# Forgetting attention and mLSTM issued as one stage, the cells of the RWKV solve moved beside the memory attention

## The reference, cut to what matters

```
one_block (forgetting attention, causal, 4 heads):
    s = q k^T * 64^-0.5 + f_t - f_s;  masked;  p = softmax(s);  out = p v
step (mLSTM, 16 chunks of 128 tokens, in sequence):
    log_d = b_t - b_s + i_s;  m_t = max(...)
    s   = (q k^T) * exp(log_d - m_t)
    num = s v + w_inter * (q C);  den = sum(s) + w_inter * (q n)
    h   = num / max(|den|, exp(-m_t));  C, n = decay * (C, n) + (w k)^T v
    then sigmoid(o) * h and an RMS norm per head
memory_attention: q of 2048 tokens against 256 memory rows, softmax, p v
rwkv7_time_mix: a delta rule; the kernel solves it by chunks of 128 and
    needs the inverse of unit lower triangular cells of 32 x 32
```

## Time and profile before

| | us |
|---|---|
| median of 3 runs (4438.66 to 4448.36) | 4440.43 |
| the profiled execution | 4424.24 |
| its span | 4422.5 |
| stage fox, from its first DMA to the next stage's first instruction (1348.8 to 1664.2) | 315.4 |
| stage rwkv_factors (1664.2 to 1837.2) | 173.0 |
| stage mlstm with the cells (1837.2 to 2122.3) | 285.1 |
| stage rwkv_chunks (2122.3 to 2352.4) | 230.1 |
| stage mem (2352.4 to 2474.7) | 122.3 |

### The profile page before, as it was taken

The page is one execution under the profiler, slowest core; times in us unless marked ns, Lnnn a source line. Parts: engine busy times, 40 slices in busy tenths (PEclk is TensorE's granted clock), DMA queues, the critical chain, the costliest instruction groups (busy, mean ns, idle before and its releaser), DMA issues. The chain is left out here.

```text
span 4422.5 us, 41472 instructions
## 1 busy us (share of the span) xinstructions
PE 3479.1 (79%) x14981; PEld 2625.0 (59%) x14981; DVE 1570.1 (36%) x2571; ACT 897.6 (20%) x1351; POOL 706.8 (16%) x731
## 2 busy tenths in 40 slices
PE   5848888799955993345796499689899686999879
PEld 2636666588843661244694288567788233666567
DVE  0113223203243445677454222356000100777613
ACT  1022222211012332201121133321001100333210
POOL 1042222111101000122341322110111000000031
PEclk7669999899987995555898699899999898999989
DMA  5232222322214401111003355322221115455354
GB/s 170 86 124 68 82 65 79 132 71 71 71 44 92 84 17 61 43 36 47 17 12 83 112 186 175 111 95 83 78 76 57 68 36 140 83 111 114 79 167 143
DMA packets 305282, 383.48 MB, mean 87 GB/s; under 512 B 83808, under 2 KB 243232, under 8 KB 290096
## 3 DMA queue, kind: packets, MB, share of 16 engines
q1 hardware_dynamic: 289144, 378.00, 29.3%
q10 hardware_dynamic: 16016, 3.95, 0.5%
HBM read 246.36 MB, written 135.53 MB: 86 GB/s over the span
## 5 line engine op out<-in xcount | busy, mean ns | idle before, releaser
L504 PE MATMUL f_psum_out<-f_x_high,f_w_high 128*128 128x512 f32 x1440 | 569.8, 396 | 97.1 <-DVE f_x_low L482 52.8
L504 PE MATMUL f_psum_out<-f_x_low,f_w_high 128*128 128x512 f32 x1440 | 567.3, 394 | 0.0
L504 PE MATMUL f_psum_out<-f_x_high,f_w_low 128*128 128x512 f32 x1440 | 566.5, 393 | 0.0
L504 PEld LDWEIGHTS f_psum_out<-f_x_high,f_w_high 128*128 128x128 f32 x1440 | 274.8, 191 | 163.4 <-issue 92.0
L504 PEld LDWEIGHTS f_psum_out<-f_x_high,f_w_low 128*128 128x128 f32 x1440 | 274.6, 191 | 57.8
L504 PEld LDWEIGHTS f_psum_out<-f_x_low,f_w_high 128*128 128x128 f32 x1440 | 274.9, 191 | 57.1
L393 PE MATMUL p_psum_proj<-p_w_high,p_h_high 128*128 128x512 f32 x512 | 219.2, 428 | 68.4 <-issue 44.7
L1032 PE MATMUL nbr_psum_o<-nbr_probT,nbr_v 128*128 128x512 f32 (+3 forms) x576 | 238.8, 496 | 18.7 <-ACT nbr_probT L1056 18.7
L393 PE MATMUL p_psum_proj<-p_w_high,p_h_low 128*128 128x512 f32 x512 | 215.1, 420 | 0.0
L393 PE MATMUL p_psum_proj<-p_w_low,p_h_high 128*128 128x512 f32 x512 | 213.8, 418 | 0.0
L490 POOL CAST f_w_high<-f_w 128x1024 fp32r<-128x1024 f32 x45 | 46.8, 1040 | 873.0 <-PE f_psum_out L504 575.3
(11 more groups left out here) (494 smaller groups left out, 6586.1 us busy)
## 6 DMA issues: line engine op xcount, KB each, us to landing
f_w<-in_w_fm SPq DMA_DIRECT2D x45, 512.0 KB, 5.4
ada_w<-in_w_ada SPq DMA_DIRECT2D x6, 2048.0 KB, 16.8
scratch_qkmT<-p_qkT_out SPq DMA_DIRECT2D x32, 384.0 KB, 3.3
scratch_z1T<-f_out SPq DMA_DIRECT2D x10, 1024.0 KB, 4.7
p_z<-scratch_z1T SPq DMA_DIRECT2D x16, 640.0 KB, 5.8
p_xt<-in_x SPq DMA_DIRECT2D x16, 512.0 KB, 4.8
p_staging<-in_w_tok SPq DMA_DIRECT2D x8, 1024.0 KB, 4.8
scratch_hT<-p_h_slot SPq DMA_DIRECT2D x16, 512.0 KB, 5.8
```

The lines of the kernel that those rows point to most:

```text
L504: last = nc.tensor.matmul(self.p_out[b][:, at], self.w_parts[b][w_part][:, k, :], self.x_parts[x_part][:, k, at], start=(k == 0 and i == 0 ...
```

## The change

Four things change. First, the engine programs of a stage become Python generators that yield a place (a number of steps), and `run_together` merges them on each engine by that number; where two have the same, the program named first goes first. Second, fox and mLSTM become one stage, all tiles named `heads_*`: chunk c of mLSTM is cut into hops at places 10c, 10c+1, ... of fox's 160 steps (`TURN = 10`). Third, to fit eight PSUM banks, fox has two banks for scores in place of three and one for units in place of two, and mLSTM has three in place of six: `psum_state` and `psum_num` share the bank of `psum_t`, `psum_inter` that of `psum_max`. Fourth, the cells are solved in the DVE program of the memory attention, two turns in each step from step 10 on, and `mem_attention` takes mLSTM's place between `rwkv_factors` and `rwkv_chunks`. The nbr stage keeps its banks and its order.

```diff
+def interleave(*programs):
+    turns = [[next(p, None), p] for p in programs]
+    while turns := [t for t in turns if t[0] is not None]:
+        turn = min(turns, key=lambda t: t[0])
+        turn[0] = next(turn[1], None)
...
-S_BUFS, M_BUFS, P_BUFS = 3, 2, 4
+P_BUFS = 4
...
+        yield -1
+        dve.wait_ge(const_ready, 1)
...
+        for s in range(n_steps + 4):
+            yield s
+            if aside:
+                aside(dve, s, n_steps)
+            for m in plan.before[s]:
+                largest(m)
+            if s >= 3 and plan.ends_group(s - 3):
+                normalise(plan.group_of(s - 3))
...
+                     extra_ones=[raw(qx[b][HD:HD + 2, :]) for b in range(2)], s_bufs=2, m_bufs=1)
...
+    run_together(nc, attention(nc, d, g, ph, plan, kT, v, 7, load_head, lambda b, q1: q1, lambda b: kT[b], d["y1T"][GW:2 * GW],
+                               aside=cells.eliminate), cells.transfers())
...
+        first = 2 * (s - self.FIRST)
+        for j in range(max(first, 0), min(first + 2, CELL - 1)):
...
+            yield self.FIRST + CELL // 2
+            sp.wait_ge(self.x_done, 1)
...
+    p_state = p_num = p_t
+    p_inter = p_max[:].rearrange("p h t -> p (h t)")
...
+    def on_tensor(pe):
+        yield -2
+        pe.wait_ge(const_in, 48)
+        pe.wait_ge(sel_ready, 1)
+        for h in range(GH):
+            last = nc.tensor.matmul(p_max[:, h, 0:NT], sel[:, h, :], carry_row[:], start=True, stop=True)
...
+            yield TURN * c + 5
+            pe.wait_ge(state_ready, c + 2)
+            pe.wait_ge(sm_ready, c + 1)
...
+            yield TURN * c + 6
+            dve.wait_ge(num_ready, c + 1)
...
-    mlstm(nc, d, g, cells)
+    mem_attention(nc, d, g, cells)
     rwkv_chunks(nc, d, g, big, to_next, cells)
...
-    fox_attention(nc, d, g)
+    ph = Phase(nc, "heads")
+    run_together(nc, fox_attention(nc, d, g, ph), mlstm(nc, d, g, ph))
+    ph.close()
     rwkv(nc, d, g)
-    mem_attention(nc, d, g)
     tile_pass_2(nc, d, g)
```

More of the change, by code:

```diff
@@ new lines, in on_sync, with load @@
+    def on_sync(sp):
+        def load(h):
+            b = h % 2
+            if h >= 2:
+                sp.wait_ge(o_ready, plan.ends[plan.group(h - 2, GROUPS - 1)])
+            load_head(sp, h, b, q1[b], q2[b], head_in[b])
+            if tables:
+                tables.load(sp, h, b)
+        yield -3
+        load(0)
+        load(1)
+        for n in range(n_groups):
+            yield plan.ends[n] + 3
+            h, q = n // GROUPS, n % GROUPS
+            at = slice(h % 2 * HD, h % 2 * HD + HD)
+            sp.wait_ge(y_ready, n + 1)
+            sp.dma_start(y_dst[h * HD:(h + 1) * HD, q * BANK:(q + 1) * BANK], y[n % 2][at, :]).then_inc(y_stored[n % 2], 16)
+            if q == GROUPS - 1 and h + 2 < plan.nh:
+                load(h + 2)
+        for b in range(2):
+            sp.wait_ge(y_stored[b], 16 * n_groups // 2)
@@ new lines, in on_scalar @@
+    def on_scalar(act):
+        yield -1
+        if key_bias:
+            act.wait_ge(key_bias.ready, 1)
+        for s in range(n_steps):
+            yield s
+            h, q, b, lo, hi, _, _ = plan.steps[s]
+            out = probT[s % P_BUFS][:, lo:hi]
+            if local_before[s + 1] > local_before[s]:
+                act.wait_ge(biased, local_before[s + 1])
+                nc.scalar.activation(out, out, ACT.Exp).then_inc(prob_ready, 1)
+            else:
+                act.wait_ge(s_ready, s + 1)
+                if s >= P_BUFS:
+                    act.wait_ge(o_ready, s - P_BUFS + 1)
+                nc.scalar.activation(out, p_s[s % s_bufs][:, lo:hi], ACT.Exp,
+                                     bias=key_bias.column(h, b) if key_bias else 0.0).then_inc(prob_ready, 1)
@@ L1026, in values @@
-            def values(s):
-                h, q, b, lo, hi, first, end = plan.steps[s]
-                n = plan.group(h, q)
-                if first and n >= 2:
-                    pe.wait_ge(y_ready, n - 1)
-                pe.wait_ge(prob_ready, s + 1)
-                nc.tensor.matmul(p_o[n % 2][:, lo:hi], v[h % 2][:, b, :], probT[s % P_BUFS][:, lo:hi],
-                                 start=first, stop=end).then_inc(o_ready, 1)
-            pe.wait_ge(ones_ready, 1)
-            pe.wait_ge(const_ready, 1)
@@ L1128 @@
+    return on_sync, on_gpsimd, on_tensor, on_scalar, on_vector
 class KeyBias:
```

727 lines of the change are left out of this document (354 added, 373 removed).

## The result

The changed kernel takes 4385.81 us (median of 4 runs, 4373.59 to 4394.18), the kernel before 4444.40 in the same comparison (4 runs, 4438.66 to 4452.22): a ratio of 0.9865, 95% interval 0.9833 to 0.9897. Forecast were 4380 us and faster. The profiled execution took 4373.59 us with a span of 4371.5.

The account below looks back on a forecast made before the run. PE was taken to bound fox, the chain inside a chunk mLSTM, and DVE mem. Merging gains 84.5 us and the cells cost mem 24, so 4440.4 - 60.5 = 4380 us, range 4305 to 4425.

Parts of the forecast that it names:

- F: Length of the merged fox and mLSTM stage, summed on PE: 516 us against 600.5 for the two before.
- Start: Merged stage before its first unit: PE waits for mLSTM's constants, issued behind both heads' loads; 50.7 us.
- Fox's own run and mLSTM's work: Items 2 and 3, PE in the merged stage: fox's run stays 285.4 us, mLSTM's matmuls add 78 us.
- One unit bank, hops: Items 4 and 5, merged stage: PE waits 53 us for the single unit bank, 32 us behind DVE's hops.
- Clock: Item 6, PE in the merged stage: five clock falls after gaps, 2 us lost in each, 10 us.
- End: Item 7, end of the merged stage: 4 us as before and 3 for the last chunk's norm and store.
- 98 us of the rest: Merged-stage time outside PE's part, used by the clock rival to set its deciding mean clock of 0.74.
- Mem: Memory attention with the cells on DVE: grows by 24 us, with 18.9 us hidden in two load waits.
- the waits for `mem_v` gone or under 1 us: Sign in mem: PE's two waits for a head's load, 9.7 us each, would be filled by the cells.
- No real overlap: Rival, merged stage: every hop finds its partner late; F = 559 us, kernel 4423 us; chance 0.12.
- Nearly all hidden: Rival, merged stage: single-bank waits and hops take turns; F = 432 us, kernel 4296 us; chance 0.20.
- The clock falls (slower): Rival, merged stage: gaps bring down PE's clock; at 0.6, F = 685 us, kernel 4548 us; chance 0.08.

Follow-up runs that it names:

- start_hop: Changed kernel with loads ordered mLSTM constants, fox's head 0, chunks 0 and 1, head 1, plus the edit of hop_split: 4332.82 us.
- hop_split: Changed kernel with the gate's reciprocal on DVE moved from place 6 to place 5: 4366.09 us.
- apart_banks: The kernel of apart, but fox has two score banks and one unit bank as in the merged stage: 4521.97 us.
- clock_fill: Changed kernel with extra PE products, their result never read, put in the seven long pauses: 4362.57 us.
- pause: The kernel of apart with two 512-element divisions on DVE ahead of step 8's units in each head: 4448.98 us.
- no_cells: Changed kernel without the cells' 62 operations, transfers kept, so the solve works on other numbers: 4387.54 us.
- apart: Changed kernel with fox (three score banks, two unit banks) and mLSTM as two stages again, cells left in mem: 4445.14 us.
- consts_first: Changed kernel with mLSTM's three constant loads issued ahead of all of fox's loads: 4370.05 us.

## Why the prediction was right, and where it was off

The forecast of the whole (4380, measured 4385.81) held, and its mechanism was in the main the one that the trace shows. That it came within 6 us is luck in part: F was forecast 20.7 us too low and mem 9.5 too high, and the medians differ by 58.6 us where the profiled executions, from which the sum was made, differ by 50.7.

1. *Start*, 50.7 us: measured 1400.24 - 1348.4 = 51.8. start_hop shows the cause, the order of the loads.
2. and 3. *Fox's own run and mLSTM's work.* The records of mLSTM's products overlap one another; counted from the start of one to the start of the next, or to its end where PE then waits, they take 78 us, as forecast, 121 ns each at the full clock (68 us for all) and the rest by the clock, below.
4. and 5. *One unit bank, hops.* By the prediction PE would wait 85 + 9.7 us (the 9.7 of the earlier trace rows are inside item 2's run); it waited 75.8, and 3.8 for `sm`. The longest stands behind place 6 and the division, as said, four times; hop_split took 15.9 of the waits away by moving one operation. So the two items came out 15 us too high. That waits of the bank and of the hops cover one another, as the lower bound has it, may be why; it is not shown.
6. *Clock*, 10 us: this is the term that was mis-sized. It counted five falls at 2 us. There were seven, of 6.8 to 17.1 us, and PE was busy in 70 of their 85 us: 35 us lost, and 5 more in a warm-up that lasts 27 us in place of 12. With 30 us more here, 10 less in item 3 (its 68 us at full clock), 15 us less of waits, and 1 more at the start and 1 less at the end, the forecast 516 becomes 521 of the 536.8 measured. Some 16 us have no term in the prediction; 9 of them may be the 55 more waits than before, at the 0.16 us each of apart_banks. clock_fill (18 us back for 36 fewer busy us in slow windows) bears out the price, and pause (four pauses, four falls) that a pause brings a fall; apart_banks and clock_fill show that shorter waits do too.
7. *End*, 7 us: 5.6 from the issue of fox's last store (1879.57) to the end of the stage.

PE's busy time (396.8 against "about 350") and the mean clock (0.84 against "above 0.85") were the two signs that showed this at once. The Trainium skill, TensorE: Matmul & The Clock Gate, section A second HAM failure mode: psum-queue depth-cycling, has it that short idle spells of PE between groups of matmuls make the clock go to and fro and cost throughput. This trace agrees, with 0.84 in the mean; the prediction put the rule under a rival of its own, all or nothing, and that rival's point of decision (a mean of 0.74) was not reached. The point itself was set too low: the "98 us of the rest" are 143 by the prediction's own items (50.7 + 53 + 32 + 7), and with them it is 0.81, not far below the 0.84 measured.

*Mem*, 24 us: measured 14.5, and 15.0 by no_cells. The operations take 32.7 us, as forecast (33.2):

```profile
L2333 DVE TENSOR_TENSOR mem_cells_x<-mem_cells_x,mem_cells_less 128x62 f32<-128x62 f32 (+15 forms) x31 | 16.4, 528 | 2.3
L2330 DVE TENSOR_TENSOR mem_cells_less<-mem_cells_low,mem_cells_x 128x62 f32<-128x62 f32 (+15 forms) x31 | 16.3, 527 | 2.9 <-issue 0.2
```

The busy time leaves nothing for the 4 us of contention with POOL's diagonals. The step that failed is their overlap in time:

```profile
2108.79 1.04 POOL L1018 TENSOR_TENSOR mem_diag<-ident,mem_neg 128x512 fp32r<-128x512 f32 x1 [7.57 <-DVE mem_neg L1123]
2111.34 0.52 DVE L2330 TENSOR_TENSOR mem_cells_less<-mem_cells_low,mem_cells_x 128x350 f32<-128x350 f32 x1
```

A diagonal starts at `neg` and ends while DVE is in the division; the cells stand behind the division, and none of the 16 diagonals runs beside one. The Trainium skill, SBUF — State Buffer, section Who interferes with whom, names the contention that the prediction priced at up to 8 us; mem does not test it, since the two never run together there. The store and reads of SP (1 us) cost nothing either. Between no_cells and the changed kernel DVE's waits for units fall from 40.6 to 20.3 us, so 20.3 of the 37.9 (32.7 and 5.2 of gaps) are hidden, about the 18.9 forecast. What remains, 17.6, is 2.6 above the 15.0. The sign "the waits for `mem_v` gone or under 1 us" failed: the two of the earlier trace rows are still there, 4.57 and 1.66 in place of 9.7 each. Head 2's load is issued at 2103.25 and PE goes on at 2116.77, 13.5 us as before. Turns 2 to 5 lengthen the group that runs meanwhile, and that is what shortens the wait; turns 6 to 9 run from 2111.34 to 2116.45, under the wait itself, and leave it as long as it is.

*The rivals.* "No real overlap" rested on mLSTM without cells at 219 us, the busy time of the cells taken off; apart measured 264.9. The mistake was mostly the banks: by the estimate under apart the cells and their read-back cost 46 us of the 66 taken off, and the shared banks, which the rival left out, bring 27. By the measured figure that rival gives F = 316.9 + 264.9 + 25 = 607. The forecast F did not rest on this figure, but the account of the gain does: of the 63.7 us some 46 are the cells that left mLSTM, against 14.5 in mem, and some 18 the merging itself, net of the shared banks. "Nearly all hidden" failed at the bank and the clock. "The clock falls (slower)" was right in kind and too large.

## What to carry to other kernels

Before merging a chain of waits into a full PE stream, list each place where PE will pause for two us or more, and price it twice: the pause, and half of the busy time until the clock is back (about 7 us after one pause in a full stream, 7 to 17 in the merged stage). Count crowded short waits as well: with none above 0.8 us they took 25 us through the clock in apart_banks. Of a small number of PSUM banks give the second to the buffer that turns over most often (here 160 units against 16 groups' sums, 39 us), and put the loads of every program that PE needs first ahead of anyone's second buffer (23 us). Where one edit both takes work out of a stage and takes banks from it, price the two apart: mLSTM alone shows 20 us gained, which by its chunks is some 46 for the cells less 27 for the banks.

## What was not expected of the hardware

In three of the twelve runs (apart, apart_banks, no_cells) the stage of the chunks took 256 us in place of 231, with the same instructions (in no_cells on other numbers). The windows of its beginning, in the changed kernel and in apart:

```profile
2194.40:2209.80 15.40, 5.92 (x26) 3.93 (x26) 12.00 (x13) 0.65 (x2) 9.45 (x28) 0.52 0.05 9
2209.80:2261.80 52.00, 51.09 (x430) 46.91 (x432) 22.71 (x50) 14.39 (x43) 16.19 (x43) 1.00 0.02 7
```

```profile
2240.60:2256.00 15.40, 5.98 (x26) 4.10 (x26) 11.98 (x13) 0.60 (x1) 9.44 (x28) 0.50 0.03 9
2256.00:2308.00 52.00, 51.53 (x228) 45.80 (x229) 11.85 (x25) 7.57 (x23) 5.62 (x17) 0.50 0.00 1
2308.00:2330.00 22.00, 22.00 (x178) 21.05 (x178) 9.38 (x23) 5.82 (x17) 9.31 (x24) 0.92 0.04 13
```

PE is as busy in the one as in the other, 98 and 99% of 52 us, but here the clock stayed at its lower level through all of it (228 matmuls in place of 430), and rose 71 us after the start of the stage in place of 15. What makes it rise late is open; no run tells it apart. It is worth knowing when a few tenths of a per cent are read from single runs: 25 us are 0.6% of this kernel, more than consts_first, hop_split or clock_fill gained. The runs of the changed kernel span 20.6 us; whether this lies behind it is open, as only one of them has a profile.

SP's queue took 15.3 to 17.6 us for one issue behind the loads of a head, in every run (16.91 above). That makes the order of issue on SP an order in time for everything behind it.
